# FFN gate and up products with x stationary, and the hidden activations transposed by DMA

## The chip, the cores and the metric

The kernel runs on one NeuronCore of one Trainium2 chip. The metric is the device time of one execution in microseconds (us), and less is better. TensorE is written PE, its weight load PEld, VectorE DVE, ScalarE ACT, GpSimd POOL and SyncE SP.

## What is computed

Two identical decoder layers with separate weights run over 256 tokens of width 1024, in float32. A layer has four attention mixers behind one input projection (`w_in`), gates (`w_gate`), branch products, an output product and then the feed-forward part (FFN), which is what the change touches. FFN_HIDDEN is 2816.

```python
hn = _rms_norm(x, ffn_norm_g[l])
x = x + (jax.nn.silu(hn @ w_ffn_gate[l]) * (hn @ w_ffn_up[l])) @ w_ffn_down[l]
```

The row factor of the RMS norm (one number for each token) is not applied to x ahead of the products. It is applied to their results, before the silu.

## The kernel before

**Weights in chunks.** All weights stream through a ring of four raw buffers `w_raw`, in chunks of 128 partitions x 2 x 512 float32 (512 KB). `CHUNKS` (L44) lists the chunks of a layer, and its index is the slot number `u` by which all engines order their work: chunk n is multiplied in slot n. SP loads chunk n when DVE is done with chunk n-4 (L576, `s_lo`). ACT makes `w_hi` by a copy that rounds to fp32r (L981 to L995, it waits until PE is done with chunk n-4), and DVE makes `w_lo = w_raw - w_hi` (L1225 to L1231). Both do so two slots ahead (`LEAD`). PE then forms three products: hi x hi, lo x hi and hi x lo. So a value is carried in two parts, and three products stand for one float32 product.

**Two ways to multiply.** In all stages but the FFN's first, `product` (L725) has x stationary (loaded as 128x128) and the weights moving, 512 columns wide. A chunk is then 12 matmuls of 512 columns, and the result has tokens on the partitions. The FFN's gate and up products (L707 to L723) have the weights stationary and x moving: a chunk is 8 matmuls with `w_hi` over 512 columns (the hi and lo parts of x side by side in `xt`) and 8 with `w_lo` over 256 columns. The result has hidden columns on the partitions and tokens along the row, which is the layout in which the down product takes it as its stationary operand. A group j of 128 gate and 128 up columns (`FC` is 128, `N_FFN` 22) takes two chunks.

**Behind each group** (steps `act`, `silu`, `hid`, `split`, L180 to L183): ACT copies the first halves of both PSUM banks to `gate_up` (L1077), DVE adds the second halves (L1305), POOL multiplies by the norm factor spread along the rows (`rows`, L1601), ACT applies Silu (L1083), DVE multiplies gate by up into `hid` (L1313), and ACT and DVE split `hid` into `ht_hi` and `ht_lo` (L1086, L1317). The factor reaches its `rows` form by a DVE copy, four matmuls with an identity and an ACT copy (L924, L1089). Two pairs of PSUM banks alternate between the groups: the products of group j+2 wait until DVE has read group j (L696 to L700).

**Order.** Each engine walks the slots in order. `PLAN` gives the slots of small steps, `RANK` their order within a slot; steps of rank 3 and more come behind the weight split of the slot. `pair f` steps transpose x for the FFN (four PE transposes each, L773) and split it (L1018, L1241); `stats f` sums the squares (L1100) and makes the norm factor.

**DMA transposes that exist before.** For mixers C and D POOL deals float32 tiles into two planes of 16-bit halves (`deal`, L1556), SP transposes each plane by DMA (`turn`, L581 to L588: two instructions of 128 x 1024 16-bit elements, issued from the same queue as the weight loads), and POOL joins the planes into float32 again (`join`, L1565).

Of the kernel before, what the change touches and what calls it, by code (L numbers as in the profile page):

```python
# [24 lines left out]
FC = 128  # L25
# [22 lines left out]
          + [("ffn", j, q) for j, q in ((0, 0), (1, 0), (0, 1), (1, 1))]  # L48
          + [("ffn", j, q) for j in range(2, N_FFN) for q in range(2)]
# [21 lines left out]
TURN_AT = {33: "C", 40: "D"}  # L71


def in_cols(g):
# [9 lines left out]
    "rows": 4, "stats": 1, "lambda": 14, "x": (0, 0, 1, 2), "f": (-2, -1, 1, 1), "m": (-1, -1, 2, 3),  # L84
# [30 lines left out]
def maps_of(mixer, n):  # L115
# [11 lines left out]
    "x0": 0, "f0": 0, "m0": 0, "proj": 4, "zg": 4, "merge": 2, "xadd": 0.5, "act": 4, "silu": 4, "hid": 4.5,  # L127
    "split": 5, "rows": 1, "Acum": 5.5, "Dp": 6, "cpv": 3.5, "sig": 4.5, "Cpv": 3, "cbuild": 1.5, "kct": 2,
# [6 lines left out]
def steps():  # L135
# [11 lines left out]
    put(U_FFN + PLAN["stats"], "stats", "f")  # L147
# [130 lines left out]
def banks_of(step):  # L278
# [61 lines left out]
def trunk_kernel(nc, x, x_t, w_in, w_gate, w_branch, w_out, w_ffn, w_ffn_down,  # L340
                 norm_g, gains, lam, cmp_pe, cmp_w, b_gate, const, masks, out):
    with ExitStack() as ctx:
# [44 lines left out]
        gate_up = place("gate_up", [P, 2, 2, SEQ], F32, at=big2)  # L387
        silu = place("silu", [P, 2, SEQ], F32, at=big2 + 16 * SEQ)
        hid = place("hid", [P, 2, SEQ], F32, at=big2 + 24 * SEQ)
        assert big2 + 32 * SEQ <= top[0]  # L390
        rows_at = big + 8 * FFN // P * SEQ
        rows = place("rows", [P, SEQ], F32, at=rows_at)
        spread = place("spread", [P, NT, P], F32, at=rows_at + 4 * SEQ)
        assert rows_at + 8 * SEQ <= end_big

# [95 lines left out]
        halves = Events(sem("gate_up_first_parts"), keys("act"))  # L491
        scaled = Events(sem("gate_up_scaled"), keys("act"))
        hid_done = Events(sem("hid_done"), keys("hid"))
        spread_done = Events(sem("rstd_spread"), keys("rows"))
# [155 lines left out]
        def _(pe):  # L650
# [20 lines left out]
            def products(l, u):  # L671
# [4 lines left out]
                else:  # L676
# [1007 lines left out]
```

## Time and profile before

| what | value |
|---|---|
| time, median of 3 runs | 844.51 us (844.47 to 844.72) |
| the profiled execution: its own time, its span | 844.52 us, 842.7 us |
| PE busy | 837.1 us (99%), 4482 matmuls |
| PE weight loads | 700.4 us (83%) |
| DVE, ACT, POOL busy | 614.2, 498.2, 291.8 us (73, 59, 35%) |
| granted TensorE clock | 1.0 in every slice |
| DMA | 157.34 MB, mean 187 GB/s |
| chain that ended last | PE 97%, DVE 1%, DMA 1%, ACT 1% |

A share of busy time says how full an engine is, not whether work waits for it. The chain that ended last goes back from the last instruction to what released each step, so its shares say on which engine time was spent that nothing else covered. A matmul's recorded duration includes its way through the pipeline, and so neighbours overlap: the distance between the starts of two groups of matmuls is what a group costs.

### The profile page before, as it was taken

To read this page: it belongs to the slowest core of one execution; us is meant where nothing else is said; L and a number is where in the kernel's file an instruction comes from. 1 tells how busy PE (TensorE), PEld (TensorE's weight loads), DVE (VectorE), ACT (ScalarE), POOL (GpSimd) and SP (SyncE) were. 2 spreads that over 40 slices of the span, in tenths; PEclk is the share of its full clock that TensorE was granted. 3 is DMA by queue.
4 is the path that set the end of the run, shared out by engine and by line. 5 is a ranking of instruction groups with operands and counts; after the bars stand their busy time and mean duration, and the time that the engine had idled before them with its cause. 6 is when DMAs were issued, how large, how long until landed. Compare 5 with 4: busy or idle time off the path is not lost.

```text
span 842.7 us, 12151 instructions
## 1 busy us (share of the span) xinstructions
PE 837.1 (99%) x4482; PEld 700.4 (83%) x4482; DVE 614.2 (73%) x933; ACT 498.2 (59%) x827; POOL 291.8 (35%) x273
## 2 busy tenths in 40 slices
PE   9999999999999999999999999999999999999998
PEld 5888888888888888888888888887888888888886
DVE  5567888758869888875455688887597698888542
ACT  6786655654467666654457775556644666666441
POOL 0078863004314444420000989530061244444100
PEclk9999999999999999999999999999999999999999
DMA  9755774554556566565565468745545566655652
GB/s 330 261 145 184 209 216 149 174 180 146 200 175 197 181 196 186 190 197 177 171 205 197 145 200 201 212 154 178 181 150 176 175 201 198 189 188 182 204 189 73
DMA packets 76890, 157.34 MB, mean 187 GB/s; under 512 B 13856, under 2 KB 16288, under 8 KB 76576
## 3 DMA queue, kind: packets, MB, share of 16 engines
q1 hardware_dynamic: 76544, 156.30, 58.6%
q8 instruction: 36, 0.59, 0.3%
q10 hardware_dynamic: 288, 0.27, 0.1%
q14 instruction: 22, 0.18, 0.1%
HBM read 153.40 MB, written 1.05 MB: 183 GB/s over the span
## 4 chain that ended last, share of the span: by engine, by line
PE 97%; DVE 1%; DMA 1%; ACT 1%; issue 0%; SPq 0%; ACTq 0%
PE acc L726 61%; PE acc L715 18%; PE acc L720 10%; PE att L806 1%; PE att L888 1%; PE att L773 1%; PE att L863 1%; DMA w_raw<-in_w_in 1%; PE att L879 1%; PE att L798 1%; PE acc L806 0%; PE acc L863 0%; PE att L847 0%; DVE xs L1300 0%; DVE w_lo L1230 0%
## 5 line engine op out<-in xcount | busy, mean ns | idle before, releaser
L1230 DVE TENSOR_TENSOR w_lo<-w_raw,w_hi 128x1024 fp32r<-128x1024 f32 (+1 forms) x276 | 375.9, 1374 | 107.5 <-ACT w_hi L995 106.0
L995 ACT ACTIVATE w_hi<-w_raw 128x1024 fp32r<-128x1024 f32 (+1 forms) x275 | 286.5, 1052 | 114.1 <-PE acc L726 87.5
L726 PE MATMUL acc<-w_hi,xt 128*128 128x512 f32 (+1 forms) x1024 | 259.2, 395 | 0.7 <-ACT w_hi L989 0.5
L726 PEld LDWEIGHTS acc<-w_hi,xt 128*128 128x128 f32 x1024 | 186.1, 188 | 38.4 <-issue 1.5
L715 PE MATMUL acc<-xt,w_hi 128*128 128x512 f32 x704 | 176.8, 393 | 0.5 <-DVE xt L1241 0.5
L1601 POOL TENSOR_TENSOR gate_up<-gate_up,rows 128x256 f32<-128x256 f32 x88 | 108.0, 1247 | 140.3 <-DVE gate_up L1305 122.6
L715 PEld LDWEIGHTS acc<-xt,w_hi 128*128 128x128 f32 x704 | 126.8, 189 | 23.5 <-issue 0.9
L726 PE MATMUL acc<-w_lo,xt 128*128 128x512 f32 (+1 forms) x512 | 135.8, 387 | 0.0
L726 PEld LDWEIGHTS acc<-w_lo,xt 128*128 128x128 f32 x512 | 96.0, 188 | 19.2
L720 PEld LDWEIGHTS acc<-xt,w_lo 128*128 128x128 f32 x704 | 96.0, 190 | 6.9
L720 PE MATMUL acc<-xt,w_lo 128*128 128x256 f32 x704 | 98.2, 283 | 0.0
L1488 POOL TENSOR_SCALAR small<-small 128x2 f32<-128x2 f32 (+4 forms) x14 | 9.3, 665 | 206.8 <-ACT sq_dump L1100 129.3
L1608 POOL TENSOR_TENSOR merged<-merged,prod 128x1024 f32<-128x1024 f32 x10 | 32.4, 3240 | 126.4 <-DVE prod L1279 125.5
L1305 DVE TENSOR_TENSOR gate_up<-acc,gate_up 128x256 f32<-128x256 f32 x88 | 33.2, 419 | 29.2 <-ACT gate_up L1077 29.2
L1077 ACT ACTIVATE gate_up<-acc 128x256 f32<-128x256 f32 x88 | 28.9, 381 | 42.8 <-PE acc L720 42.8
L726 PE MATMUL acc<-w_hi,ht_hi 128*128 128x512 f32 x176 | 47.8, 391 | 0.0
L726 PE MATMUL acc<-w_lo,ht_hi 128*128 128x512 f32 x176 | 47.6, 389 | 0.0
L726 PE MATMUL acc<-w_hi,ht_lo 128*128 128x512 f32 x176 | 47.6, 390 | 0.0
L1053 ACT ACTIVATE eb<-eb,small 128x128 f32<-128x128 f32 x64 | 28.3, 443 | 25.8 <-DVE small L1367 25.8
L1317 DVE TENSOR_TENSOR ht_lo<-hid,ht_hi 128x256 fp32r<-128x256 f32 x44 | 40.0, 910 | 0.0
L726 PEld LDWEIGHTS acc<-w_hi,ht_lo 128*128 128x128 f32 x176 | 33.1, 188 | 6.9
L726 PEld LDWEIGHTS acc<-w_lo,ht_hi 128*128 128x128 f32 x176 | 33.1, 188 | 6.9
(188 smaller groups left out, 828.7 us busy)
## 6 DMA issues: line engine op xcount, KB each, us to landing
w_raw<-in_w_ffn SPq DMA_DIRECT2D x88, 512.0 KB, 4.0
w_raw<-in_w_gate SPq DMA_DIRECT2D x64, 512.0 KB, 4.1
w_raw<-in_w_ffn_down SPq DMA_DIRECT2D x44, 512.0 KB, 4.1
w_raw<-in_w_in SPq DMA_DIRECT2D x39, 512.0 KB, 5.0
w_raw<-in_w_branch SPq DMA_DIRECT2D x16, 512.0 KB, 3.8
w_raw<-in_w_out SPq DMA_DIRECT2D x16, 512.0 KB, 3.5
bg<-in_b_gate SPq DMA_DIRECT2D x8, 512.0 KB, 5.5
w_raw<-in_w_in SPq DMA_DIRECT2D x8, 396.0 KB, 3.6
```

The source lines that it names most:

```text
L715: pe.matmul(acc[bank0 + i][:, :], wh4[:, k, i * FC:(i + 1) * FC], xt[:, 4 * b + k, :, :].rearrange("p i t -> p (i t)"), start=first and k ...
L720: mm = pe.matmul(acc[bank0 + i][:, 0:SEQ], wl4[:, k, i * FC:(i + 1) * FC], xt_hi[:, 4 * b + k, :], start=False, stop=last and k == 3)
L726: return pe.matmul(acc[bank0 + t][:, 0:N], x_part[:, k0 + k, t * P:(t + 1) * P], w_part[:, k, 0:N], start=first, stop=last)
L995: act.activation(w_hi[:, n % WR, :, 0:N], w_raw[:, n % RAW, :, 0:N], copy).then_inc(s_hi, 1)
L1053: ins = act.activation(e_map(e)[:, cols], e_map(e)[:, cols], ACT.Exp, scale=-1.0, bias=nbias[r][:, j:j + 1], accum_out=sums[r][:, j:j + 1])
L1077: ins = act.activation(gate_up[:, a % 2, i, :], acc[bank_pair(l, step) + i][:, 0:SEQ], copy)
L1230: dve.tensor_tensor(w_lo[:, n % WR, :, 0:N], w_raw[:, n % RAW, :, 0:N], w_hi[:, n % WR, :, 0:N].bitcast(F32), ALU.subtract).then_inc(s_lo, 1)
L1305: ins = dve.tensor_tensor(gate_up[:, a % 2, i, :], acc[bank_pair(l, step) + i][:, SEQ:], gate_up[:, a % 2, i, :], ALU.add)
L1317: dve.tensor_tensor(ht_lo[:, a, :], hid[:, a % 2, :], ht_hi[:, a, :].bitcast(F32), ALU.subtract).then_inc(ht_lo_done.now(step), 1)
L1488: settled(pool.tensor_scalar(dst, sumsq, 1.0 / n, EPS, ALU.mult, ALU.add))
L1601: ins = pool.tensor_tensor(gate_up[:, a % 2, i, :], gate_up[:, a % 2, i, :], rows[:, :], ALU.mult)
L1608: pool.tensor_tensor(merged[:, :, cols], merged[:, :, cols], prod[:, :, half_], ALU.add).then_inc(pool_done.now(step), 1)
```

## The change

`FC` becomes 256, so the FFN has 11 groups of 256 gate and 256 up columns, each of four chunks (still 44 chunks a layer and the same bytes). The FFN's own matmul code goes, and its chunks take the common path with x stationary: 12 matmuls of 512 columns. A PSUM bank then holds 128 tokens x (256 gate, 256 up) columns, and the norm factor is one number for each partition: ACT applies it inside the Silu, DVE inside the product of gate and up. The copies, additions and scalings of `gate_up` go, and so do the `rows` matmuls and copies.

The hidden values now have tokens on the partitions, and the down product wants the transpose. For each group POOL deals `hid` into 16-bit planes (`hdeal`: two copies of 128x512 16-bit elements), SP issues two DMA transposes of 128x512 16-bit elements (`turn_hid`, its place in SP's order eight slots behind the group's last chunk), POOL joins (`hjoin`: two copies of 128x512), and ACT and DVE split the joined 128x512 float32 tile in slot done+6. The first two groups are interleaved by halves, the transposes `f` 2 and 3 move from slot 1 of the FFN to slots 2 and 3, and `stats f` from 1 to 3.

```diff
-FC = 128
+FC = 256
...
-          + [("ffn", j, q) for j, q in ((0, 0), (1, 0), (0, 1), (1, 1))]
-          + [("ffn", j, q) for j in range(2, N_FFN) for q in range(2)]
+          + [("ffn", j, q) for half in range(2) for j in range(2) for q in (2 * half, 2 * half + 1)]
+          + [("ffn", j, q) for j in range(2, N_FFN) for q in range(4)]
...
-TURN_AT = {33: "C", 40: "D"}
+TURN_AT = {33: "C", 40: "D"} | {CHUNKS.index(("ffn", j, 3)) + 9: j for j in range(N_FFN)}
...
-    "rows": 4, "stats": 1, "lambda": 14, "x": (0, 0, 1, 2), "f": (-2, -1, 1, 1), "m": (-1, -1, 2, 3),
+    "stats": 1, "stats_f": 3, "lambda": 14, "x": (0, 0, 1, 2), "f": (-2, -1, 2, 3), "m": (-1, -1, 2, 3),
...
-        done = CHUNKS.index(("ffn", j, 1)) + 1
-        for n, kind in ((0, "act"), (2, "silu"), (2, "hid"), (3, "split")):
+        done = CHUNKS.index(("ffn", j, 3)) + 1
+        for n, kind in ((0, "act"), (0, "hdeal"), (3, "hjoin"), (6, "split")):
             put(done + n, kind, j)
...
+        silu = place("silu", [P, 2, NT, FC], F32, at=big2)
+        hid = place("hid", [P, 2, NT, FC], F32, at=big2 + 16 * FC)
+        assert big2 + 32 * FC <= top[0]
+        tail = big + 8 * FFN // P * SEQ
+        hid_halves = place("hid_halves", [P, 2, NT, 2, FC], U16, at=tail)
+        hid_halves_t = place("hid_halves_t", [P, 2, NT, 2, 2, P], U16, at=tail + 16 * FC)
+        hid_t = place("hid_t", [P, 2, SEQ], F32, at=tail + 32 * FC)
...
+            def turn_hid(l, j):
+                sp.wait_ge(hid_dealt.sem, hid_dealt.at(l, ("hdeal", j)))
+                if j > 1:
+                    sp.wait_ge(hid_joined.sem, hid_joined.at(l, ("hjoin", j - 2)))
+                for t in range(NT):
+                    sp.dma_start_transpose(hid_halves_t[:, j % 2, t, :, :, :].rearrange("p s k q -> p (s k) q"),
+                                           hid_halves[:, j % 2, t, :, :].rearrange("p s c -> p (s c)")
+                                           ).then_inc(s_hturn[j % 2], 16)
...
-                        turn(l, TURN_AT[u])
+                        (turn if TURN_AT[u] in ("C", "D") else turn_hid)(l, TURN_AT[u])
...
-                    if u == U_FFN + 6 and l + 1 < DEPTH:
+                    if u == U_FFN + 12 and l + 1 < DEPTH:
...
-                               "out": (a == 0, a == 3), "ffn": (b == 0, b == 1),
+                               "out": (a == 0, a == 3), "ffn": (b == 0, b == 3),
...
-                src = {"in": ("x", b) if a == 0 else None, "ffn": None, "gate": None,
+                src = {"in": ("x", b) if a == 0 else None, "ffn": ("f", b) if a == 0 else None, "gate": None,
...
-                    pe.wait_ge(ht_hi_done.sem, ht_hi_done.at(l, ("split", 2 * a + 1)))
-                    pe.wait_ge(ht_lo_done.sem, ht_lo_done.at(l, ("split", 2 * a + 1)))
+                    pe.wait_ge(ht_hi_done.sem, ht_hi_done.at(l, ("split", a)))
+                    pe.wait_ge(ht_lo_done.sem, ht_lo_done.at(l, ("split", a)))
...
-                if kind == "ffn":
-                    for k in range(4):
-                        if a == 0 and k % 2 == 0:
-                            ready = ("pair", ("f", 2 * b + k // 2))
-                            pe.wait_ge(hi_done.sem, hi_done.at(l, ready))
-                            pe.wait_ge(read_dve.sem, read_dve.at(l, ready))
-                        for i in range(2):
-                            pe.matmul(acc[bank0 + i][:, :], wh4[:, k, i * FC:(i + 1) * FC],
-                                      xt[:, 4 * b + k, :, :].rearrange("p i t -> p (i t)"), start=first and k == 0, stop=False)
-                    pe.wait_ge(s_lo, n + 1)
-                    for k in range(4):
-                        for i in range(2):
-                            mm = pe.matmul(acc[bank0 + i][:, 0:SEQ], wl4[:, k, i * FC:(i + 1) * FC], xt_hi[:, 4 * b + k, :],
-                                           start=False, stop=last and k == 3)
-                    mm.then_inc(s_ch, 1)
-                    return
-
...
-                        elif kind == "rows":
-                            bank_free(ll, step)
-                            pe.wait_ge(spread_done.sem, spread_done.at(ll, step))
-                            for t in range(NT):
-                                mm = pe.matmul(att[:, OB, t * P:(t + 1) * P], spread[:, t, :], ident, start=True, stop=True)
-                            mm.then_inc(att_done.now(step), 1)
...
-                    act.wait_ge(s_ch, chunk(l, CHUNKS.index(("ffn", a, 1)) + 1))
+                    act.wait_ge(s_ch, chunk(l, CHUNKS.index(("ffn", a, 3)) + 1))
+                    if a == 0:
+                        act.wait_ge(pool_done.sem, pool_done.at(l, ("stats", "f")))
                     if a > 1:
-                        act.wait_ge(hid_done.sem, hid_done.at(l, ("hid", a - 2)))
+                        act.wait_ge(dve_acc.sem, dve_acc.at(l, ("act", a - 2)))
                     elif l:
                         act.wait_ge(s_cw, 16 * (l + 1))
-                    for i in range(2):
-                        ins = act.activation(gate_up[:, a % 2, i, :], acc[bank_pair(l, step) + i][:, 0:SEQ], copy)
-                    ins.then_inc(halves.now(step), 1)
-                elif kind == "silu":
-                    act.wait_ge(scaled.sem, scaled.at(l, ("act", a)))
-                    if a > 1:
-                        act.wait_ge(hid_done.sem, hid_done.at(l, ("hid", a - 2)))
-                    act.activation(silu[:, a % 2, :], gate_up[:, a % 2, 0, :], ACT.Silu).then_inc(act_misc.now(step), 1)
+                    for t in range(NT):
+                        ins = act.activation(silu[:, a % 2, t, :], acc[bank_pair(l, step) + t][:, 0:FC], ACT.Silu,
+                                             scale=xr["f"][:, t:t + 1])
+                    ins.then_inc(silu_done.now(step), 1)
                 elif kind == "split":
-                    act.wait_ge(hid_done.sem, hid_done.at(l, ("hid", a)))
-                    act.activation(ht_hi[:, a, :], hid[:, a % 2, :], copy).then_inc(ht_hi_done.now(step), 1)
...
-                    dve.wait_ge(halves.sem, halves.at(l, step))
-                    for i in range(2):
-                        ins = dve.tensor_tensor(gate_up[:, a % 2, i, :], acc[bank_pair(l, step) + i][:, SEQ:],
-                                                gate_up[:, a % 2, i, :], ALU.add)
+                    dve.wait_ge(silu_done.sem, silu_done.at(l, step))
+                    if a > 1:
+                        dve.wait_ge(hid_dealt.sem, hid_dealt.at(l, ("hdeal", a - 2)))
+                    for t in range(NT):
+                        ins = dve.scalar_tensor_tensor(out=hid[:, a % 2, t, :], in0=acc[bank_pair(l, step) + t][:, FC:],
+                                                       scalar=xr["f"][:, t:t + 1], in1=silu[:, a % 2, t, :],
+                                                       op0=ALU.mult, op1=ALU.mult)
                     ins.then_inc(dve_acc.now(step), 1)
-                elif kind == "hid":
-                    dve.wait_ge(act_misc.sem, act_misc.at(l, ("silu", a)))
-                    if a > 1:
-                        dve.wait_ge(ht_hi_done.sem, ht_hi_done.at(l, ("split", a - 2)))
-                        dve.wait_ge(ht_lo_done.sem, ht_lo_done.at(l, ("split", a - 2)))
-                    dve.tensor_tensor(hid[:, a % 2, :], silu[:, a % 2, :], gate_up[:, a % 2, 1, :], ALU.mult
-                                      ).then_inc(hid_done.now(step), 1)
                 elif kind == "split":
                     dve.wait_ge(ht_hi_done.sem, ht_hi_done.at(l, step))
-                    dve.tensor_tensor(ht_lo[:, a, :], hid[:, a % 2, :], ht_hi[:, a, :].bitcast(F32), ALU.subtract
+                    dve.tensor_tensor(ht_lo[:, 2 * a:2 * a + 2, :], hid_t[:, :, :],
+                                      ht_hi[:, 2 * a:2 * a + 2, :].bitcast(F32), ALU.subtract
                                       ).then_inc(ht_lo_done.now(step), 1)
...
-                        elif kind == "act":
-                            pool.wait_ge(dve_acc.sem, dve_acc.at(l, step))
-                            if a == 0:
-                                pool.wait_ge(read_act.sem, read_act.at(l, ("rows", None)))
-                            for i in range(2):
-                                ins = pool.tensor_tensor(gate_up[:, a % 2, i, :], gate_up[:, a % 2, i, :], rows[:, :], ALU.mult)
-                            ins.then_inc(scaled.now(step), 1)
+                        elif kind == "hdeal":
+                            pool.wait_ge(dve_acc.sem, dve_acc.at(l, ("act", a)))
+                            for t in range(NT):
+                                ins = pool.tensor_copy(hid_halves[:, a % 2, t, :, :],
+                                                       hid[:, a % 2, t, :].bitcast(U16).rearrange("p (c s) -> p s c", s=2))
+                            ins.then_inc(hid_dealt.now(step), 1)
+                        elif kind == "hjoin":
+                            pool.wait_ge(s_hturn[a % 2], turned(l, a))
+                            if a:
+                                pool.wait_ge(ht_lo_done.sem, ht_lo_done.at(l, ("split", a - 1)))
+                            for t in range(NT):
+                                dst = hid_t[:, :, t * P:(t + 1) * P].bitcast(U16)
+                                ins = pool.tensor_copy(dst.rearrange("p k (q s) -> p k q s", s=2),
+                                                       hid_halves_t[:, a % 2, t, :, :, :].rearrange("p s k q -> p k q s"))
+                            ins.then_inc(hid_joined.now(step), 1)
...
-        "w_ffn": np.stack([np.asarray(w).reshape(L, 2, 4, P, N_FFN, FC) for w in (w_ffn_gate, w_ffn_up)], axis=6)
-                   .transpose(0, 4, 1, 3, 2, 6, 5).reshape(L, N_FFN, 2, P, 2, NC), "w_ffn_down": w_ffn_down,
+        "w_ffn": np.stack([np.asarray(w).reshape(L, 4, 2, P, N_FFN, FC) for w in (w_ffn_gate, w_ffn_up)], axis=6)
+                   .transpose(0, 4, 1, 3, 2, 6, 5).reshape(L, N_FFN, 4, P, 2, NC), "w_ffn_down": w_ffn_down,
```

## Rows read from the trace of the kernel before

**Rows 1.** The page: busy time, and the chain that ended last.
```profile
PE 837.1 (99%) x4482; PEld 700.4 (83%) x4482; DVE 614.2 (73%) x933; ACT 498.2 (59%) x827; POOL 291.8 (35%) x273
...
PE 97%; DVE 1%; DMA 1%; ACT 1%; issue 0%; SPq 0%; ACTq 0%
```
**Rows 2.** Timeline of PE, layer 0, steady FFN to down: start, us, instruction.
```profile
253.68 2.00 PE L715 MATMUL acc<-xt,w_hi 128*128 128x512 f32 x8
...
359.83 2.00 PE L715 MATMUL acc<-xt,w_hi 128*128 128x512 f32 x8
361.67 1.12 PE L720 MATMUL acc<-xt,w_lo 128*128 128x256 f32 x8
362.62 1.09 PE L726 MATMUL acc<-w_hi,ht_hi 128*128 128x512 f32 x4
...
365.37 1.07 PE L726 MATMUL acc<-w_hi,ht_hi 128*128 128x512 f32 x4
...
411.62 0.60 PE L773 MATMUL att<-cst,xs 128*128 128x128 f32 x4
```
**Rows 3.** Timeline of PE, layer 0, from output chunks into the FFN.
```profile
231.54 0.60 PE L773 MATMUL att<-cst,xs 128*128 128x128 f32 x4
231.90 2.09 PE L726 MATMUL acc<-w_hi,xt 128*128 128x512 f32 x8
...
237.93 1.98 PE L715 MATMUL acc<-xt,w_hi 128*128 128x512 f32 x8
...
240.69 1.03 PE L773 MATMUL att<-cst,xs 128*128 128x128 f32 x8
...
244.78 2.06 PE L715 MATMUL acc<-xt,w_hi 128*128 128x512 f32 x8 [0.26 <-DVE xt L1241]
...
250.43 0.61 PE L924 MATMUL att<-cst,spread 128*128 128x128 f32 x4
250.80 2.10 PE L715 MATMUL acc<-xt,w_hi 128*128 128x512 f32 x8
```
**Rows 4.** Timeline of PE, layer 1: first FFN chunk, first down chunk.
```profile
654.78 1.98 PE L715 MATMUL acc<-xt,w_hi 128*128 128x512 f32 x8
...
779.50 1.09 PE L726 MATMUL acc<-w_hi,ht_hi 128*128 128x512 f32 x4
```
**Rows 5.** Timeline of the engines behind one FFN group, 262 to 269 us.
```profile
262.06 2.00 PE L715 MATMUL acc<-xt,w_hi 128*128 128x512 f32 x8
...
262.26 0.66 ACT L1077 ACTIVATE gate_up<-acc 128x256 f32<-128x256 f32 x2 [0.81 <-PE acc L720]
...
262.81 1.07 ACT L995 ACTIVATE w_hi<-w_raw 128x1024 fp32r<-128x1024 f32 x1
...
264.48 1.76 DVE L1230 TENSOR_TENSOR w_lo<-w_raw,w_hi 128x1024 fp32r<-128x1024 f32 x1
```
**Rows 6.** Groups by line and shape: busy us, mean ns, then idle before.
```profile
L1556 POOL COPY halves_in<-proj 128x512 uint16<-128x512 uint16 x4 | 4.4, 1110 | 0.0
...
L1565 POOL COPY qkt<-halves_t 128x1024 uint16<-128x1024 uint16 x8 | 11.2, 1431 | 5.1 <-issue 5.0
...
L1241 DVE SCALAR_TENSOR_TENSOR xt<-att,gt,xt 128x256 fp32r<-128x256 f32 x24 | 10.3, 478 | 10.3 <-ACT xt L1018 10.3
```
**Rows 7.** Timeline of SP's queue: issue start, us, of the DMA transposes.
```profile
113.51 4.10 SPq L587 DMA_TRANSPOSE halves_t<-halves_in  x2
...
507.65 6.90 SPq L587 DMA_TRANSPOSE halves_t<-halves_in  x2
...
509.14 5.41 SPq L587 DMA_TRANSPOSE halves_t<-halves_in  x1
```
**Rows 8.** Landing of all eight DMA transposes (`halves_t`).
```profile
DMA to landing us min/median/max: 4.9/6.4/9.5
```
**Rows 9.** Landing of the weight loads (`w_raw`): 262 to 362 us.
```profile
DMA to landing us min/median/max: 3.3/3.7/4.9
```
**Rows 10.** The same from 505 to 520 us, beside the transposes.
```profile
DMA to landing us min/median/max: 3.5/5.1/6.7
```

More of the change, by code:

```diff
@@ L126 @@
 RANK = {
-    "x0": 0, "f0": 0, "m0": 0, "proj": 4, "zg": 4, "merge": 2, "xadd": 0.5, "act": 4, "silu": 4, "hid": 4.5,
-    "split": 5, "rows": 1, "Acum": 5.5, "Dp": 6, "cpv": 3.5, "sig": 4.5, "Cpv": 3, "cbuild": 1.5, "kct": 2,
+    "x0": 0, "f0": 0, "m0": 0, "proj": 4, "zg": 4, "merge": 2, "xadd": 0.5, "act": 4,
+    "split": 5, "Acum": 5.5, "Dp": 6, "cpv": 3.5, "sig": 4.5, "Cpv": 3, "cbuild": 1.5, "kct": 2,
     "x": 0.5, "Asp": 6, "Bpv": 4.5, "ck": 1, "cv": 1.5, "cs": 3.5, "prep": 0.5, "Csm": 3, "Dpv": 4.5,
@@ L146, in steps @@
     put(PLAN["stats"], "stats", "x")
-    put(U_FFN + PLAN["stats"], "stats", "f")
+    put(U_FFN + PLAN["stats_f"], "stats", "f")
     for g in range(N_IN):
@@ L293, in banks_of @@
         return (S1,)
-    if kind in ("o", "rows"):
+    if kind == "o":
         return (OB,)
@@ L386, in trunk_kernel @@
         eb_more = place("eb_more", [P, 4, 384], F32, at=big2)
[L387 to L394, printed above, removed]
+        silu = place("silu", [P, 2, NT, FC], F32, at=big2)
[5 more added lines that the diff above has]
+        hid_t = place("hid_t", [P, 2, SEQ], F32, at=tail + 32 * FC)
+        assert tail + 40 * FC <= end_big
         qkt = [place(f"qkt{i}", [P, 4, SEQ], F32) for i in range(2)]
@@ L490, in trunk_kernel @@
         ht_lo_done = Events(sem("ht_lo_done"), keys("split"))
[L491 to L494, printed above, removed]
+        silu_done = Events(sem("silu_done"), keys("act"))
+        hid_dealt = Events(sem("hid_dealt"), keys("hdeal"))
+        hid_joined = Events(sem("hid_joined"), keys("hjoin"))
         proj_out = Events(sem("proj_read"), keys("proj"))
         act_misc = Events(sem("scalar_small"), [s for s in ORDER if s[0] in (
-            "stats", "lambda", "prep", "ngate", "kcprep", "cs", "sig", "silu", "sm")])
+            "stats", "lambda", "prep", "ngate", "kcprep", "cs", "sig", "sm")])
         dve_acc = Events(sem("acc_read_dve"), keys("zg", "merge", "xadd", "act"))
@@ L503, in trunk_kernel @@
         s_turn = sem("halves_transposed")
+        s_hturn = [sem(f"hid_halves_transposed{i}") for i in range(2)]
         merged_done = Events(sem("merged_done"), [("merge", (3, 1))])
@@ L533, in weight, with turned @@
             return [(w_ffn_down[l, 2 * a * P:(2 * a + 2) * P, b * NC:(b + 1) * NC], slice(0, NC))]
+        def turned(l, what):
+            if what in ("C", "D"):
+                return 16 * NT * (2 * l + "CD".index(what) + 1)
+            return 16 * NT * (l * len(range(what % 2, N_FFN, 2)) + what // 2 + 1)
         def raw_value(n):
@@ L1070, in do @@
                 elif kind == "act":
-                    act.wait_ge(s_ch, chunk(l, CHUNKS.index(("ffn", a, 1)) + 1))
+                    act.wait_ge(s_ch, chunk(l, CHUNKS.index(("ffn", a, 3)) + 1))
+                    if a == 0:
+                        act.wait_ge(pool_done.sem, pool_done.at(l, ("stats", "f")))
                     if a > 1:
-                        act.wait_ge(hid_done.sem, hid_done.at(l, ("hid", a - 2)))
+                        act.wait_ge(dve_acc.sem, dve_acc.at(l, ("act", a - 2)))
                     elif l:
                         act.wait_ge(s_cw, 16 * (l + 1))
-                    for i in range(2):
-                        ins = act.activation(gate_up[:, a % 2, i, :], acc[bank_pair(l, step) + i][:, 0:SEQ], copy)
-                    ins.then_inc(halves.now(step), 1)
-                elif kind == "silu":
-                    act.wait_ge(scaled.sem, scaled.at(l, ("act", a)))
-                    if a > 1:
-                        act.wait_ge(hid_done.sem, hid_done.at(l, ("hid", a - 2)))
-                    act.activation(silu[:, a % 2, :], gate_up[:, a % 2, 0, :], ACT.Silu).then_inc(act_misc.now(step), 1)
-                elif kind == "split":
-                    act.wait_ge(hid_done.sem, hid_done.at(l, ("hid", a)))
-                    act.activation(ht_hi[:, a, :], hid[:, a % 2, :], copy).then_inc(ht_hi_done.now(step), 1)
-                elif kind == "rows":
-                    act.wait_ge(att_done.sem, att_done.at(l, step))
-                    act.activation(rows[:, :], att[:, OB, 0:SEQ], copy).then_inc(read_act.now(step), 1)
+                    for t in range(NT):
+                        ins = act.activation(silu[:, a % 2, t, :], acc[bank_pair(l, step) + t][:, 0:FC], ACT.Silu,
+                                             scale=xr["f"][:, t:t + 1])
+                    ins.then_inc(silu_done.now(step), 1)
+                elif kind == "split":
+                    act.wait_ge(hid_joined.sem, hid_joined.at(l, ("hjoin", a)))
+                    act.activation(ht_hi[:, 2 * a:2 * a + 2, :], hid_t[:, :, :], copy).then_inc(ht_hi_done.now(step), 1)
                 elif kind == "pair":
@@ L1559, in _ @@
                         elif kind == "join":
-                            pool.wait_ge(s_turn, 32 * (2 * l + "CD".index(a) + 1))
+                            pool.wait_ge(s_turn, turned(l, a))
                             last = {"C": ("z", PAIRS["A"] - 1), "D": ("sm", ("B", PAIRS["B"] - 1))}[a]
```

6 lines of the change are left out of this document (removed).

## The prediction

> **What bounds the kernel now.** I read the page first: PE is busy 99% of the span, and the chain that ended last is PE for 97% [rows 1]. DVE, at 73%, is next, and a page-wide share does not say whether it ever held PE up. So I went to PE's timeline in the FFN, where the reader should look at the distance between the starts of equal groups, not at their durations. From 253.68 to 359.83 us lie 38 FFN chunks without an idle note: 106.15 / 38 = 2.793 us each. From 365.37 to 411.62 lie 17 down chunks: 46.25 / 17 = 2.721 us each [rows 2]. Both kinds push the same 6,144 columns through PE (8 x 512 + 8 x 256 against 12 x 512); the one with fewer, longer matmuls is 0.073 us cheaper. Inside an FFN chunk the eight 512-column matmuls take 361.67 - 359.83 = 1.84 us (0.230 each) and the eight of 256 columns 362.62 - 361.67 = 0.95 us (0.119 each), where half of a down chunk's 2.721 / 12 = 0.227 would be 0.113 [rows 2]. PE bounds this stage by its own stream, so only what changes that stream, or a new wait in it, moves the time.
>
> The FFN stage runs from 237.93 to 362.62 (124.69 us) in layer 0 and from 654.78 to 779.50 (124.72 us) in layer 1 [rows 2 to 4]. Of the 124.69, 44 x 2.793 = 122.9 are chunks and 1.8 is the rest: from the eight transposes at 240.69 to the chunk at 244.78 pass 4.09 us, which is 1.30 over a chunk and holds a stall of 0.26 on DVE's `xt`; the four `rows` matmuls cost 0.37 (250.43 to 250.80), and the chunk behind them takes 253.68 - 250.80 = 2.88, 0.09 over the others, so 0.46 [rows 2, 3].
>
> **The PE stream after.** 44 chunks a layer stay. Each takes the path that the down chunks take: 44 x 0.073 = 3.2 us less a layer. The `rows` matmuls go: 0.46. The eight transposes of `f` 2 and 3 become two insertions of four. One such insertion is seen at 231.54: 0.36 to the next chunk, and by the same 0.09 behind it, 0.45; two make 0.90 in place of 1.30, if the stall is gone: 0.40. Sum 4.06 a layer, 8.1 us in all. The profiled execution took 844.52, and the median is 844.51, so the sum is made against the same number: 836.4.
>
> **Is the stall at the start gone?** With S the start of the FFN, `f` 3 is transposed in slot 3, at about S + 3 x 2.72 + 0.45 = S + 8.6, landing in PSUM by S + 9. In front of ACT's part of `f` 3 stand `f` 2 (to about S + 7), the two squares of `stats f` and one `w_hi` copy of 1.07 [rows 5]; for the squares I allow 2.2, two copies' worth. ACT's part ends by about S + 11.3 and DVE's, two of 0.478 [rows 6] behind one `w_lo`, by S + 12.6. PE wants it in slot 5, S + 14.5. Cover 1.9 us; each us past it costs 1 us a layer. The first result, group 0, is done at S + 17.3 and must be read by slot 8, S + 22.7: two Silu in the place of two copies of 0.66 together, two DVE products of 0.478, and one activation table load, for which I allow up to 2 us. That is 3.8 of 5.4.
>
> **Behind the groups.** T is the end of a group's last chunk; a group now lasts 4 x 2.721 = 10.9 us. ACT starts 0.2 behind the chunk's end and needs 0.66 for two reads of PSUM [rows 5]; DVE's two products are like L1241, 0.478 each [rows 6], so `hid` stands at T + 1.9, or T + 3.7 if a `w_lo` of 1.76 [rows 5] is in front. PE asks for these banks at T + 10.9, so this is hidden. The work removed (copies, additions, POOL's scaling) was on engines off the path and is costed at nothing.
>
> POOL deals with two copies of 1.11 [rows 6]: T + 4.1. SP's pair of DMA transposes has as its nearest rows the pairs of double size: SP is held 4.1 to 6.9 us [rows 7]. The bytes halve, so from 2.0, if the time follows the bytes, to 6.9, if it does not; I take 3.5, the half of the upper. Landing is 4.9 to 9.5 behind the issue, and the second issue comes 1.5 behind the first (509.14 - 507.65), so the pair lands within 4.9 to 11.0 [rows 7, 8]; I take 7.9, the full-size median 6.4 and 1.5: T + 12.0. POOL joins with two copies of half the width of L1565, so 0.7 to 1.4 each [rows 6], say 1.4 for both: T + 13.4. ACT comes to the split of this group in slot done+6, behind its weight copy, which may start when chunk done+4 is finished: T + 13.6 + 1.1 = T + 14.7. So ACT would not wait. With every upper bound at once (3.7 + 2.2 + 11.0 + 2.8) the join ends at T + 19.7 and ACT waits 5 us; then its next weight copy ends at about T + 21.5, and PE wants that chunk (done+9) at T + 24.5. Still nothing.
>
> What is queued behind SP's new wait is the load of chunk done+8. In [rows 5] the `w_lo` that frees a raw buffer ends at 266.24, 4.2 behind the start of the PE chunk at 262.06, and belongs to the chunk three further on; so load done+8 is due at T + 2.7 + 4.2 = T + 6.9. The transposes hold SP until T + 4.1 + 3.5 = T + 7.6, at worst T + 11.0 (T + 12.8 with a late `hid`). The load lands in 3.7, and in up to 6.7 beside transposes [rows 9, 10]; ACT can use it from T + 13.6, and PE needs its copy only at T + 21.8. The expected case is 7.6 + 6.7 = 14.3, which takes 0.7 from a slack of some 7 us of the weights ahead of PE. The worst, 12.8 + 6.7 = 19.5 and a copy of 1.1, still ends 1.2 ahead of PE. The last group's split comes near T + 17 and is wanted by the eleventh down chunk, T + 27.
>
> The Trainium skill, VectorE: DVE Perf Modes, section on the three transpose paths, gives 1309 ns for a 128x128 block through the DMA crossbar against 390 on TensorE, and its rules advise TensorE where the result may go to PSUM. An estimate from that page: eight blocks a group, 10.5 us if they go one by one, which would fill the group's 10.9 us and feed rival B. The trace disagrees: sixteen blocks hold SP for 4.1 to 6.9 us, 0.26 to 0.43 a block [rows 7].
>
> **Rivals.** A, the forecast: PE's stream shortens and all else stays hidden, 836.4, of itself 835.6 to 838.0 (the bounds of the insertions and a stall of up to 0.8 a layer).
>
> B, slower: SP becomes the bound. Its queue is in order and each group holds one pair and four loads. If a pair kept SP until it has landed, and the landing did not shrink with the bytes, a pair takes up to 11.0, and four issues at about 0.35 (an allowance) add 1.4: 12.4 a group against 10.9, 1.5 x 22 groups = 33 us, less the 8.1: 869. It decides from a pair of 9.5 us on; at 9.9 the gain is gone (0.4 x 22 = 8.8). For it: such a pair took 6.9 at double size, with weight loads in the same queue. Against it: 6.9 is the largest of that, and half the bytes are moved.
>
> C, the 0.073 us is not a matter of 16 against 12 matmuls but of something else in the FFN stage that remains. Then only 2 x 0.86 = 1.7 us go: 842.8. Against it: the down chunks follow the last FFN chunk directly and at once run at the other pace, on the same path of the code [rows 2]. The Trainium skill, TensorE: Matmul & The Clock Gate, section Back-to-back issue gap, gives 518 and 262 cycles for 512 and 256 columns; by these an FFN chunk shrinks from 6,240 to 6,216 cycles, an estimate of 0.01 us, 0.9 us over all. The trace speaks against the page: 0.119 us for 256 columns is more than half of 0.227.
>
> D, the covers at the start of the FFN fail (1.9 us for `f` 3, 1.6 for group 0), or ACT and POOL meet late once per group in part: 1 to 3 us a layer return, 838 to 842.
>
> **How the numbers follow.** A 0.83, B 0.05, C 0.03, D 0.06, and 0.03 for less than 835.6. The range 835.6 to 839.2 holds A and the near part of D. About 1.7 us (0.2%) is what can be told from no change. Faster by more: A, D and the remainder, 0.92; within: C, 0.03; slower: B, 0.05.
>
> **What would show it.** Right: FFN chunks 2.72 us apart in both layers, no idle note on PE in the FFN but at most one at its start, no `rows` matmuls, an FFN stage of 120.6 us a layer. The pair of transposes holds SP under 7 us, and the weight loads land in under 7. Wrong: FFN chunks at 2.79 (C); PE waiting on `w_hi` or `w_lo` once a group, with SP's loads issued late behind transposes (B); PE idle in slots 5 or 8 (D); ACT idle before the split, waiting for POOL, is allowed up to 5 us and costs nothing until then.

## The result, and the profile after

The changed kernel takes 836.65 us (median of 4 runs, 836.24 to 836.82) against 844.49 us: a ratio of 0.9906 with a 95% interval of 0.9889 to 0.9923, 7.8 us less. The forecast was 836.4.

The busy times after, and the chain that ended last, answer to [rows 1]:

```profile
PE 829.7 (99%) x4122; PEld 681.1 (82%) x4122; DVE 555.9 (67%) x821; ACT 465.8 (56%) x715; POOL 263.5 (32%) x273
...
PE 98%; DMA 1%; issue 0%; SPq 0%; ACT 0%; DVE 0%
```

PE did 360 matmuls fewer and was busy 7.4 us less; its share stays at 99%, so its stream still is the time. DVE lost 58 us of work and ACT 32. The 8.1 us that the span lost are accounted for below without them: before the change the FFN stage held one wait of PE for DVE, 0.26 us at its start in each layer, and its end has nothing to do with the work removed (see e10). PE's timeline in layer 0, from the last output chunk through the FFN into the down product, answers to [rows 2, 3]:

```profile
235.22 2.09 PE L721 MATMUL acc<-w_hi,xt 128*128 128x512 f32 x8
...
238.05 1.98 PE L721 MATMUL acc<-w_hi,xt 128*128 128x512 f32 x8
...
243.50 0.60 PE L768 MATMUL att<-cst,xs 128*128 128x128 f32 x4
...
246.68 0.60 PE L768 MATMUL att<-cst,xs 128*128 128x128 f32 x4
...
249.87 1.98 PE L721 MATMUL acc<-w_hi,xt 128*128 128x512 f32 x8
...
358.67 1.07 PE L721 MATMUL acc<-w_hi,ht_hi 128*128 128x512 f32 x4
```

Neither these rows nor those left out between them have an idle note, and in layer 1 it is the same. From 249.87 to 358.67 lie 40 chunks: 108.80 / 40 = 2.720 us each, where [rows 2] had 2.793. An insertion of four transposes costs 246.68 - 243.50 - 2.72 = 0.46. The stage lasts 358.67 - 238.05 = 120.62 us against 124.69, and 120.62 in layer 1 (650.79 to 771.41): 4.1 us less in each, 8.2 together. The spans differ by 842.7 - 834.6 = 8.1.

Behind the group that ended at 304.27 (T, where the next chunk's matmuls start), the timelines of POOL, ACT and SP show the new path:

```profile
306.28 2.16 POOL L1576 COPY hid_halves<-hid 128x512 uint16<-128x512 uint16 x2 [3.14 <-DVE hid L1291]
312.82 1.29 POOL L1585 COPY hid_t<-hid_halves_t 128x512 uint16<-128x512 uint16 x2 [4.38 <-DMA hid_halves_t<-hid_halves]
...
319.03 0.62 ACT L1073 ACTIVATE ht_hi<-hid_t 128x512 fp32r<-128x512 f32 x1
```

```profile
308.46 2.52 SPq L599 DMA_TRANSPOSE hid_halves_t<-hid_halves  x2
311.04 8.17 SPq L583 DMA_DIRECT2D w_raw<-in_w_ffn  x4
```

The join is done at 314.1, T + 9.8 (13.4 was expected), and ACT comes to it at T + 14.8 (14.7 was expected). All 44 transposes, their hold of SP in ns and their landing, and then the landing of the weight loads from 262 to 362 us:

```profile
L599 SPq DMA_TRANSPOSE hid_halves_t<-hid_halves x44: 1194/1244/1300, 259.5 to 776.8; - x44
...
DMA to landing us min/median/max: 2.4/3.6/5.6
```

```profile
DMA to landing us min/median/max: 3.1/3.9/5.5
```

The weights land 0.2 us later than in [rows 9] in the median, against a slack of several us.

### The profile page after: what moved, and what is told of

It reads as the page before. It is cut to its first block, busy times and chain, and to the rows that moved or that the text cites. A ratio compares the mean times of both kernels' runs of the same rounds, so it can differ in the third digit from the quotient of the medians.

```text
span 834.6 us, 11178 instructions
## 1 busy us (share of the span) xinstructions
PE 829.7 (99%) x4122; PEld 681.1 (82%) x4122; DVE 555.9 (67%) x821; ACT 465.8 (56%) x715; POOL 263.5 (32%) x273
## 4 chain that ended last, share of the span: by engine, by line
PE 98%; DMA 1%; issue 0%; SPq 0%; ACT 0%; DVE 0%
PE acc L721 90%; PE att L801 1%; PE att L883 1%; PE att L768 1%; PE att L858 1%; DMA w_raw<-in_w_in 1%; PE att L874 1%; PE att L793 1%; PE acc L801 0%; PE acc L858 0%; PE att L842 0%; PE att L896 0%; PE att L960 0%; PE att L951 0%; PE att L843 0%
## 5 line engine op out<-in xcount | busy, mean ns | idle before, releaser
L721 PE MATMUL acc<-w_hi,xt 128*128 128x512 f32 (+1 forms) x1728 | 433.5, 393 | 0.5 <-ACT xt L1007 0.5
L721 PEld LDWEIGHTS acc<-w_hi,xt 128*128 128x128 f32 x1728 | 318.2, 188 | 65.1 <-ACT w_hi L984 0.9
L721 PE MATMUL acc<-w_lo,xt 128*128 128x512 f32 (+1 forms) x864 | 229.8, 388 | 0.0
L721 PEld LDWEIGHTS acc<-w_lo,xt 128*128 128x128 f32 x864 | 162.0, 188 | 32.9
L1576 POOL COPY hid_halves<-hid 128x512 uint16<-128x512 uint16 x44 | 45.6, 1064 | 66.7 <-DVE hid L1291 66.7
L1585 POOL COPY hid_t<-hid_halves_t 128x512 uint16<-128x512 uint16 x44 | 35.3, 831 | 95.2 <-DMA hid_halves_t<-hid_halves 80.8
L721 PEld LDWEIGHTS acc<-w_hi,ht_hi 128*128 128x128 f32 x176 | 32.9, 188 | 6.7
L1291 DVE SCALAR_TENSOR_TENSOR hid<-acc,small,silu 128x256 f32<-128x256 f32 x44 | 19.3, 479 | 25.9 <-ACT silu L1068 25.9
L1466 POOL TENSOR_TENSOR small<-small 128x2 f32<-128x2 f32 (+4 forms) x14 | 34.9, 2496 | 1.2
L1246 DVE SCALAR_TENSOR_TENSOR zg<-acc,small,bg 128x512 f32<-128x512 f32 x32 | 22.4, 741 | 0.9 <-PE acc L721 0.8
```

The source lines that it names most:

```text
L721: return pe.matmul(acc[bank0 + t][:, 0:N], x_part[:, k0 + k, t * P:(t + 1) * P], w_part[:, k, 0:N], start=first, stop=last)
L1246: ins = dve.scalar_tensor_tensor(out=zg[:, t, i, c * NC:(c + 1) * NC], in0=acc[bank_pair(l, step) + t][:, :], scalar=xr["x"][:, t:t + 1], ...
L1291: ins = dve.scalar_tensor_tensor(out=hid[:, a % 2, t, :], in0=acc[bank_pair(l, step) + t][:, FC:], scalar=xr["f"][:, t:t + 1], in1=silu[:, ...
L1466: return pool.tensor_tensor(dst, dst, exps_, ALU.pow)
L1576: ins = pool.tensor_copy(hid_halves[:, a % 2, t, :, :], hid[:, a % 2, t, :].bitcast(U16).rearrange("p (c s) -> p s c", s=2))
L1585: ins = pool.tensor_copy(dst.rearrange("p k (q s) -> p k q s", s=2), hid_halves_t[:, a % 2, t, :, :, :].rearrange("p s k q -> p k q s"))
```

## The experiments

All are edits of the changed kernel, and their times stand against its 836.65 us. The kernel before, run along with them, took 844.36 to 844.51.

**e1: the w_lo products in halves of 256 columns.**

```diff
+                    if kind == "ffn" and narrow and not last:
+                        for c in (slice(0, N // 2), slice(N // 2, N)):
+                            mm = pe.matmul(acc[bank0 + t][:, c], x_part[:, k0 + k, t * P:(t + 1) * P],
+                                           w_part[:, k, c], start=first, stop=last, skip_group_check=True)
+                        return mm
```

> The changed kernel, but in the FFN gate and up chunks each hi x w_lo matmul of 512 columns is issued as two of 256 (all but the last of each tile in a group's last chunk: 3.5 of 4 a chunk on average). x stays stationary, columns and values are the same. Theory (the gain is a price for each narrow matmul: 0.119 us against half of 0.227): 3.5 x (0.238 - 0.227) = 0.040 us a chunk, x 88 = 3.5 us, so about 840.2. Rival (the gain comes from x being stationary, and the number of matmuls does not count): no change, 836.7.

Measured: 842.32 us, 5.7 more. PE's timeline of two chunks:

```profile
263.56 2.00 PE L726 MATMUL acc<-w_hi,xt 128*128 128x512 f32 x8
265.40 1.12 PE L723 MATMUL acc<-w_lo,xt 128*128 128x256 f32 x8
266.36 2.00 PE L726 MATMUL acc<-w_hi,xt 128*128 128x512 f32 x8
268.20 1.11 PE L723 MATMUL acc<-w_lo,xt 128*128 128x256 f32 x8
```

A full narrow chunk costs 266.36 - 263.56 = 2.80 us, as before the change, with x stationary. Chunks in which 3.5 of 4 matmuls with `w_lo` are halved, on average, give back 0.073 x 88 x 3.5 / 4 = 5.6 us. So the chunk's price came from the 16 matmuls with eight narrow ones, not from what is stationary. My 3.5 us priced only the narrow ones (0.96 against 0.91 us). The eight wide ones between them also grow, from 1.81 to 1.84, as in [rows 2]: about a third of the difference.

**e2: all products of the FFN chunks in halves.** The condition of e1 without `narrow and not last`. The halves carry start marks of their own, which changes the first sums; only its time is read.

> The changed kernel with every matmul of the FFN gate and up chunks issued as two of 256 columns: 24 matmuls a chunk in place of 12, x stationary. Theory (a price for each narrow matmul, 0.119 against 0.1134 us): 24 x 0.0057 = 0.136 us a chunk, x 88 = 12 us, so about 848.6. Rival (what is stationary decides): 836.7. A third: below some width the weight load sets the pace, then more than 0.119 for each, and over 850.

Measured: 851.06 us, 14.4 more. PE's timeline, eight `w_lo` halves and the sixteen `w_hi` halves behind them:

```profile
258.67 1.12 PE L723 MATMUL acc<-w_lo,xt 128*128 128x256 f32 x8
259.63 2.08 PE L723 MATMUL acc<-w_hi,xt 128*128 128x256 f32 x16
261.55 1.12 PE L723 MATMUL acc<-w_lo,xt 128*128 128x256 f32 x8
```

Sixteen take 1.92 us (259.63 to 261.55), 0.120 each; 24 make 2.88 a chunk, 0.16 over 2.72, x 88 = 14.1. So the price of a narrow matmul holds and is a little larger than the 0.119 of the expectation, and the time lies in the range of the third theory, over 850. What sets the price is not shown. The view of two stretches of 16 and of 8 matmuls, the first from e2 and the second, with 512 columns, from the changed kernel (length, then PE busy, PEld busy, DVE, ACT, POOL, the granted clock, DMA share and GB/s), has the weight loads without a gap in the first only:

```profile
259.63:261.55 1.92, 1.92 (x18) 1.92 (x17) 0.99 (x2) 1.06 (x1) 1.39 (x2) 1.00 0.51 74
304.27:306.08 1.81, 1.81 (x9) 1.50 (x8) 0.74 (x2) 1.61 (x3) 0.00 (x0) 1.00 0.72 285
```

Eight transposes of 128 columns, in e10, take 0.79 us (240.47 to 241.26), 0.099 each, again with PEld busy for all of it. That fits a pace set by the weight load, which the third theory named; no run tests it alone.

**e3: the transposes on PE.** Deal, DMA transposes and join go.

```diff
-        for n, kind in ((0, "act"), (0, "hdeal"), (3, "hjoin"), (6, "split")):
+        for n, kind in ((0, "act"), (3, "hpt"), (3, "split")):
...
+                        elif kind == "hpt":
...
+                                    mm = pe.transpose(att[:, TP, (2 * k + t) * P:(2 * k + t + 1) * P],
+                                                      hid[:, a % 2, t, k * P:(k + 1) * P], ident)
```

> The changed kernel, but hid is transposed by PE: four transposes of 128x128 a group into PSUM in slot done+3, split from there by ACT and DVE; no deal, no DMA transposes, no join. Theory (PE's stream is the bound, all of the DMA path is beside it): 22 insertions of 0.45 us = 9.9 us more, about 846.5, which is more than the kernel before. Rival (the DMA path costs something that is hidden in the sum, so taking it away gives part back): under 844.

Measured: 846.47 us, ratio to the kernel before 1.0026 (1.0016 to 1.0036). PE's timeline:

```profile
269.16 0.60 PE L907 MATMUL att<-cst,hid 128*128 128x128 f32 x4
...
272.34 1.98 PE L707 MATMUL acc<-w_hi,xt 128*128 128x512 f32 x8
```

An insertion costs 272.34 - 269.16 - 2.72 = 0.46 us, x 22 = 10.1; 9.8 were measured. So x stationary alone, with the transposes in PE's stream, is slower than the kernel before, and taking the DMA path away gave back 0.3 us at most.

**e4, e5, e6: each pair of DMA transposes issued 4, 2 and 3 times**, the copies into spare room; POOL waits for all.

```diff
+                for r in range(3):
+                    for t in range(NT):
+                        dst = spare[:, j % 2, r, t, :, :, :] if r < 2 else spare2[:, j % 2, r - 2, t, :, :, :]
+                        sp.dma_start_transpose(dst.rearrange("p s k q -> p (s k) q"),
+                                               hid_halves[:, j % 2, t, :, :].rearrange("p s c -> p (s c)")
+                                               ).then_inc(s_hturn[j % 2], 16)
```

> The changed kernel with each pair of DMA transposes issued four times (three times into spare room; POOL waits for all). One pair holds SP 2.5 us after the change, so four hold it 10.0, and with four weight loads of 0.33 a group needs 11.3 us of SP against 10.88 of PE. Theory (SP's queue becomes the bound only when pair and loads exceed the group's time): 22 x 0.45 = 10 us more, 846 to 850. Rival (the DMA engines or late joins bind earlier): over 860. Rival (SP's time does not matter, loads have slack for all of it): 836.7.

Measured: 911.81 us, 75 more: a clear miss, and in the range of the rival with late joins. SP's timeline and POOL's, one group:

```profile
299.43 2.60 SPq L601 DMA_TRANSPOSE hid_halves_t<-hid_halves  x2
...
302.07 7.92 SPq L607 DMA_TRANSPOSE spare<-hid_halves  x6
...
310.04 2.00 SPq L585 DMA_DIRECT2D w_raw<-in_w_ffn  x4
311.30 1.28 POOL L1593 COPY hid_t<-hid_halves_t 128x512 uint16<-128x512 uint16 x2 [11.90 <-DMA spare<-hid_halves]
...
312.52 1.17 POOL L1584 COPY hid_halves<-hid 128x512 uint16<-128x512 uint16 x2
313.72 2.52 SPq L601 DMA_TRANSPOSE hid_halves_t<-hid_halves  x2
```

SP's loads are done at 312.04, yet the next transpose starts at 313.72, right behind POOL's deal. It is a loop: hold 10.6 (299.43 to 309.99), landing 1.3, join 1.2, deal 1.2, and again. POOL's order has join(j) ahead of deal(j+1), and SP's next pair waits for that deal. The group lasts 14.3 us: (14.3 - 10.9) x 22 = 75. SP's occupancy alone would have been 10.6 + 2.0 = 12.6, an estimate of 38 us.

> Each pair of DMA transposes issued twice. e4 (four times) took 911.8 and showed a group of 14.2 us, made up of SP held 10.4, 1.3 until the last transpose has landed, join 1.28 and the next group's deal 1.17, since POOL's order puts join(j) ahead of deal(j+1) and SP's transposes wait for that deal. Theory (this loop binds once hold + 1.3 + 2.45 exceeds 10.88, so from a hold of 7.1): at twice, 5.0 + 1.3 + 2.45 = 8.8, no change, 836.7. Rival (extra DMA traffic costs in proportion: 75 us for three extra pairs): about 861.

Measured: 836.34 us, no change. SP is held twice as long (5.1 us, 320.39 to 325.52), at no cost.

> Each pair issued three times. Theory (the loop): hold 7.5 to 7.8 + 1.3 + 2.45 = 11.3 to 11.6 against 10.88, so 0.4 to 0.7 x 22 = 9 to 15 us more: 846 to 852. Rival (SP's occupancy alone, as in the prediction's B: 7.8 + four loads of 0.5 = 9.8 under 10.88): no change, 836.7. Rival (proportional to traffic): about 886.

Measured: 854.6 us, 18.0 more, just above my band and far from both rivals. From 291.76 to 338.41 lie four groups, 11.66 us each in the mean; 0.78 x 22 = 17. Three of them last 11.5, the sum of the loop, and one, in which the transposes held SP 8.5 us, 12.2. SP's timeline of one group:

```profile
326.96 2.52 SPq L600 DMA_TRANSPOSE hid_halves_t<-hid_halves  x2
329.52 5.20 SPq L605 DMA_TRANSPOSE spare<-hid_halves  x4
334.77 2.00 SPq L584 DMA_DIRECT2D w_raw<-in_w_ffn  x4
338.41 2.58 SPq L600 DMA_TRANSPOSE hid_halves_t<-hid_halves  x2
```

SP is free from 336.77 on and waits 1.6 us for the deal: occupancy (9.8 us) does not bind, the loop does.

**e7: e4 with the join behind the next deal.**

```diff
-        for n, kind in ((0, "act"), (0, "hdeal"), (3, "hjoin"), (6, "split")):
+        for n, kind in ((0, "act"), (0, "hdeal"), (5, "hjoin"), (6, "split")):
```

> e4 (each pair four times) with the join moved from slot done+3 to done+5, so that POOL deals group j+1 before it waits for the transposes of group j. Theory (the loop through POOL's order binds e4): it is broken, and what is left is SP's 10.4 + 2.0 = 12.4 a group and the DMA engines (0.88 busy over 14.24 us in e4, so 12.5 us a group): 22 x 1.6 = 36 us over the changed kernel, about 873. Rival (POOL's order does not matter): 912 as e4.

Measured: 901.4 us, 10 under e4. The loop is gone: SP has no gap left. SP's timeline:

```profile
325.09 2.71 SPq L601 DMA_TRANSPOSE hid_halves_t<-hid_halves  x2
327.84 8.43 SPq L607 DMA_TRANSPOSE spare<-hid_halves  x6
336.32 2.00 SPq L585 DMA_DIRECT2D w_raw<-in_w_ffn  x4
338.42 3.17 SPq L601 DMA_TRANSPOSE hid_halves_t<-hid_halves  x2
```

But SP is held 11.2 to 12.0 by the same eight transposes, not 10.4, and a group takes 13.7 us (297.40 to 338.42 for three). The DMA engines are 0.91 busy over these groups, against 0.87 in e4's (299.43 to 313.72); that they push back is my reading, not shown by itself. The direction was right, the 873 was not.

**e8, e9, e11: the transposes later in SP's order**, at index 14, 13 and 11 in place of 9.

```diff
-TURN_AT = {33: "C", 40: "D"} | {CHUNKS.index(("ffn", j, 3)) + 9: j for j in range(N_FFN)}
+TURN_AT = {33: "C", 40: "D"} | {CHUNKS.index(("ffn", j, 3)) + 14: j for j in range(N_FFN)}
```

> The changed kernel with the DMA transposes five slots later in SP's order (index 14 in place of 9): issued at about T + 18.0, landed T + 22.5, joined T + 23.8, and ACT, which does the split of group j ahead of the weight copy of chunk done+9, is done with that copy at T + 25.5. PE wants it at T + 24.5. Theory (ACT's wait costs nothing until it has eaten the lead of the weights): here it is just over, 1 us a group, some 22 us: 850 to 865. Rival (a late join costs from the first us of ACT's wait on, 9 us a group): over 1000. Rival (no cost): 836.7.

Measured: 924.15 us, 87 more, far over the expected range. The engines' timeline over one group:

```profile
309.33 2.52 SPq L599 DMA_TRANSPOSE hid_halves_t<-hid_halves  x2
...
315.17 1.27 POOL L1585 COPY hid_t<-hid_halves_t 128x512 uint16<-128x512 uint16 x2 [12.25 <-DMA hid_halves_t<-hid_halves]
...
316.48 0.63 ACT L1073 ACTIVATE ht_hi<-hid_t 128x512 fp32r<-128x512 f32 x1 [9.48 <-POOL hid_t L1585]
317.01 1.99 ACT L984 ACTIVATE w_hi<-w_raw 128x1024 fp32r<-128x1024 f32 x2
...
318.10 2.92 PE L721 MATMUL acc<-w_hi,xt 128*128 128x512 f32 x8 [3.44 <-ACT w_hi L984]
...
319.34 4.52 SPq L583 DMA_DIRECT2D w_raw<-in_w_ffn  x4
319.62 2.00 ACT L984 ACTIVATE w_hi<-w_raw 128x1024 fp32r<-128x1024 f32 x2
...
321.15 2.35 DVE L1214 TENSOR_TENSOR w_lo<-w_raw,w_hi 128x1024 fp32r<-128x1024 f32 x2
...
323.95 2.60 SPq L599 DMA_TRANSPOSE hid_halves_t<-hid_halves  x2
```

Another loop, of 14.6 us: transposes and landing until 315.17, join, split, four weight copies, DVE's `w_lo` from the last of them (done at 323.50), and SP's next pair stands behind a load that waits for this `w_lo`. My expectation had followed one pass with its slack; it did not ask when the next pass can begin.

> As e8, but one slot earlier (index 13): joined near T + 21.1, the weight copy of chunk done+9 done near T + 22.8, 1.7 us ahead of PE's want at T + 24.5, while ACT waits some 6 us a group. Theory (cover): no change, 836.7. Rival (any wait of ACT reaches PE): over 860.

Measured: 885.03 us, 48 more; a miss too (groups of 13.2 us, from 278.82 to 344.82 for five). By the code, with one slot less one copy leaves the loop.

> The changed kernel with the transposes at index 11 in SP's order (14 took 924.1, 13 took 885.0, groups of 14.6 and 13.2 us). Theory (a loop: SP's turn of group j+1 stands behind a weight load, which waits for weight copies that ACT makes only after it has split group j, which waits for join(j); index 14 has four such copies in the loop, 13 three): here one is left, so 5.7 until the join + 1.3 + 0.5 for ht_hi + one copy 1.0 and its w_lo 1.2 and the issue, some 10 us, under 10.88: no change, 836.7. Rival (each slot of lateness costs, 39 us from 13 to 14 and 48 before): over 850.

Measured: 836.61 us: no change, as the loop theory says.

**e12: index 13, with the split at slot done+9.**

```diff
-        for n, kind in ((0, "act"), (0, "hdeal"), (3, "hjoin"), (6, "split")):
+        for n, kind in ((0, "act"), (0, "hdeal"), (3, "hjoin"), (9, "split")):
```

> Index 13 as in e9, with the split of hid moved from slot done+6 to done+9. The transposes and the join are as late as in e9, but the weight copies on which SP's next turn depends now stand ahead of ACT's wait. Theory (the loop, not the lateness, cost the 48 us of e9): no change against the changed kernel, 836.7. Rival (late transposes cost by themselves, or PE then waits for the last split in the down product): over 845.

Measured: 836.54 us. SP's timeline:

```profile
296.63 2.50 SPq L599 DMA_TRANSPOSE hid_halves_t<-hid_halves  x2
...
307.51 2.52 SPq L599 DMA_TRANSPOSE hid_halves_t<-hid_halves  x2
```

The pairs are 10.88 us apart, at the same place in SP's order as in e9. The 48 us were the loop's; this lateness by itself is free.

**e10: the first two groups in plain order, the transposes of f 2 and 3 and `stats f` back in slot 1.**

> The changed kernel with the FFN's first two groups not interleaved (chunks (0,0) to (0,3), then (1,0) to (1,3)), the transposes f 2 and 3 back in slot 1 and stats f in slot 1, as before the change. f 3 is then wanted in slot 3 in place of 5. From the kernel before: DVE finished f 3 about 3.9 us behind the start of these transposes, with the squares ahead of it on ACT. Theory (the interleaving is what removes the start stall): the transposes are at S + 2.7, f 2 ready near S + 6, wanted at S + 6.4; f 3 ready near S + 6.9, wanted at S + 9.1: no stall here either, since a chunk now needs one pair and not two; 836.7, within 0.5. Rival (the stall returns): 0.3 to 1 us a layer, 837.3 to 838.7, with an idle note on PE in slot 2 or 3.

Measured: 836.47 us. The timelines of PE and DVE:

```profile
240.47 1.03 PE L767 MATMUL att<-cst,xs 128*128 128x128 f32 x8
...
243.58 1.65 DVE L1224 SCALAR_TENSOR_TENSOR xt<-att,gt,xt 128x256 fp32r<-128x256 f32 x4
...
244.10 1.98 PE L720 MATMUL acc<-w_hi,xt 128*128 128x512 f32 x8
```

One insertion of eight costs 244.10 - 240.47 - 2.72 = 0.91 against 2 x 0.46, and there is no stall. So neither the interleaving nor the later slots are needed to be rid of the stall of 0.26. That a chunk now needs one pair of f tiles and not two, as the expectation has it, is not what does it either. DVE does four tiles, and f 2 is the first two of them. In the kernel before they started at 243.77:

```profile
243.77 1.65 DVE L1241 SCALAR_TENSOR_TENSOR xt<-att,gt,xt 128x256 fp32r<-128x256 f32 x4
```

PE began at 244.78, behind the first two; the last two, f 3, were done at 245.42, before the four matmuls ahead of their use had ended (244.78 + 4 x 0.23 = 245.70). So the stall was for f 2 alone. In e10 DVE's f 2 is done near 244.45, an estimate from these 1.65 us, and PE begins the chunk at 244.10. It can, because the common path first takes the four products with the high part of x, which is ACT's, and waits for DVE only ahead of the low part (L731 of the changed kernel); the FFN's own code waited for both parts ahead of its first matmul (L712 and L713 of the kernel before).

No version here beats the changed kernel by more than can be told.

## Why the prediction was right, point by point

**The chunk price.** 0.073 us a chunk was forecast and 0.073 came; e1 brought it back with x still stationary, so rival C falls. Its origin was only half named: the narrow matmuls' own price is two thirds, the wide ones between them are the rest (e1), and a stream of narrow ones alone shows 0.120 each (e2). Why a narrow one costs more than half of a wide one stays open; the weight load's pace is the rival that no run excludes.

**The `rows` matmuls and the start.** 0.46 and 0.40 a layer were forecast, and the sum of 4.06 measured 4.07 (124.69 - 120.62). D fell with its stall absent. The stall's cover was credited to the moved slots, and they are enough for it: in the changed kernel DVE was done with f 2 at 245.87 and PE wanted it at 249.87. But e10 shows that they are not needed. The order of the products in the common path is enough too, and it is not in the prediction.

**The hidden path.** The deal took 2.2 as forecast and SP was held 2.5 (3.5 taken). The pair landed 4.4 us behind its issue (308.46 to 312.82), under the lower bound of 4.9, where 7.9 was taken, so the join was done at T + 9.8 (13.4 taken). Both errors are on the safe side. That nothing of it reached PE was right, and e5 shows it by doubling the transposes for nothing.

**Where the reasoning was weak.** Rival B was priced by SP's occupancy, with its turning point at a pair of 9.5 us. The loop through POOL turns at 10.88 - 1.3 - 2.4, about 7.2, and e6, with 7.8, lost 18 us. Also the sentence that with all upper bounds at once PE still does not wait was a sum along one pass, and it is wrong. The deal of a group stands behind the join of the group before, so with the prediction's own upper bounds the loop is 2.2 (deal) + 11.0 (until the pair has landed) + 2.8 (join) = 16.0 us against 10.88, an estimate of 5.1 x 22 = 113 us more. In the changed kernel the same steps took 2.2 + 4.4 + 1.3 = 7.9 us. The 7.9 to 8.1 us of the forecast stand; the safety that it claimed did not, and that the loop stayed short was luck, as the argument did not contain this sum.

## What to carry to other kernels

Where PE's stream is the bound, count matmuls by their width, and price both widths and the change between them from start to start. Before work is called hidden, close the loops through the engines that work in order: sum every step from one group's wait to the same wait of the next group and compare that with the group's period; slack along one pass says nothing about it. A loop can be opened by moving one step in one engine's order (e12: 48 us for a changed slot number), without making anything faster.

## What the runs showed of the hardware beyond this

In the changed kernel a DMA transpose of 128 x 512 16-bit elements held SP 1.24 us (1.19 to 1.30), the first and the second of a pair alike. In the kernel before, at twice the width, the first of each of the four pairs held SP 1.24 to 1.45 us and the second 2.8 to 5.4. So the hold of the first did not follow the bytes; what made the second long is not shown.

The granted clock fell behind some stalls. In e8, behind 3.44 us without a matmul, it was 0.69 in the first 2.72 us and then 0.50, which is 1.2 of 2.4 GHz, and full again from 322.53 on. The length of the stall alone did not decide it: in e9 it was 0.59 behind a stall of 2.16 us (314.09 to 317.30) and stayed 1.00 behind one of 2.23 (340.11 to 342.90). The view of stretches (PE busy, PEld, DVE, ACT, POOL, then the granted clock, DMA share and GB/s):

```profile
318.10:320.82 2.72, 2.72 (x8) 2.16 (x9) 2.72 (x4) 2.72 (x5) 0.00 (x0) 0.69 0.20 56
320.82:322.53 1.71, 1.71 (x6) 1.32 (x4) 1.71 (x4) 0.79 (x1) 0.00 (x0) 0.50 0.95 264
322.53:325.28 2.75, 2.75 (x13) 2.27 (x12) 0.97 (x1) 0.00 (x0) 0.00 (x0) 1.00 0.91 285
```

The chunk behind the stall in e8 took 322.53 - 318.10 = 4.43 us in place of 2.72: 1.7 us more on top of the stall of 3.4.
